# Input x loaded in column halves around the first weight slab, with matmuls of constants on TensorE until it is in

## The reference

```python
h = rmsnorm(x, norm_g) @ w_in            # x: 544 x 1024, w_in: 1024 x 3080
gb, gc, hv, q, k, v, fl = jnp.split(h, splits, axis=-1)
q = rmsnorm(q.reshape(bsz, t, N_HEADS_B, HEAD_DIM), q_g)
k = rmsnorm(k.reshape(bsz, t, N_HEADS_B, HEAD_DIM), k_g)
logf = jax.nn.log_sigmoid((fl + b_f).astype(jnp.float32))
# sample group: keys, values and log forgets of 16 pages per sequence come from paged pools
lf_all = jnp.concatenate([logf_pool[page_table].reshape(bsz, p_len, h), logf_new], axis=1)
c = jnp.cumsum(lf_all, axis=1)
```

## Time and profile before

| | |
|---|---|
| median of 3 runs | 1461.29 us (1457.95 to 1469.23) |
| span of the profiled execution | 1458.5 us |
| PE busy | 1395.5 us (96%) |
| DVE, ACT, POOL busy | 721.0, 488.2, 603.2 us |
| DMA | 191.60 MB, mean 131 GB/s |

### The profile page before, as it was taken

The page is one execution under the profiler, slowest core; times in us unless marked ns, Lnnn a source line. Parts: engine busy times, 40 slices in busy tenths (PEclk is TensorE's granted clock), DMA queues, the critical chain, the costliest instruction groups (busy, mean ns, idle before and its releaser), DMA issues.

```text
span 1458.5 us, 34454 instructions
## 1 busy us (share of the span) xinstructions
PE 1395.5 (96%) x13989; PEld 1303.2 (89%) x13989; DVE 721.0 (49%) x1258; ACT 488.2 (33%) x718; POOL 603.2 (41%) x337
## 2 busy tenths in 40 slices
PE   6998998988999999999999999998999999999998
PEld 5896767767899999999999998867999999999998
DVE  5646888873535444014443367667365430144411
ACT  4375333322233222312223352237433321222221
POOL 3322332322335554445543464432255554355431
PEclk9999999998999999999999999999999999999999
DMA  6417899978322322332312546642223223322122
GB/s 185 131 54 243 289 336 319 364 267 276 120 74 77 96 83 75 88 115 83 89 55 64 147 132 162 161 118 68 61 88 96 84 76 90 101 87 86 54 84 74
DMA packets 245642, 191.60 MB, mean 131 GB/s; under 512 B 11970, under 2 KB 204947, under 8 KB 245451
## 3 DMA queue, kind: packets, MB, share of 16 engines
q1 hardware_dynamic: 244273, 187.71, 42.0%
q0 software_dynamic: 656, 2.13, 0.5%
q10 hardware_dynamic: 605, 0.24, 0.1%
HBM read 173.03 MB, written 6.04 MB: 123 GB/s over the span
## 4 chain that ended last, share of the span: by engine, by line
PE 73%; DVE 3%; ACT 1%; issue 1%; POOL 1%; DMA 0%; DVEq 0%; ACTq 0%; POOLq 0%
PE banks L1823 65%; PE banks L2265 2%; PE banks L2089 1%; PE banks L1840 1%; PE banks L2211 1%; PE banks L2028 1%; DVE k_grp L1317 0%; PE banks L1970 0%; PE banks L2268 0%; POOL sb L706 0%; DMA u_sh<-u 0%; POOL u_sh L790 0%; PE banks L2217 0%; PE banks L1857 0%; PE banks L2061 0%
## 5 line engine op out<-in xcount | busy, mean ns | idle before, releaser
L685 POOL TENSOR_TENSOR w_l<-w_raw,w_h 128x1024 fp32r<-128x1024 f32 (+2 forms) x195 | 439.5, 2255 | 400.7 <-ACT w_h L835 380.7
L1823 PE MATMUL banks<-xa_h,w_h 128*128 128x272 f32 x1856 | 388.1, 290 | 4.1 <-DVE tmp L1650 3.3
L1823 PE MATMUL banks<-xa_h,w_l 128*128 128x272 f32 x1856 | 384.5, 289 | 0.0
L1823 PE MATMUL banks<-xa_l,w_h 128*128 128x272 f32 x1856 | 383.1, 288 | 0.0
L1823 PEld LDWEIGHTS banks<-xa_h,w_h 128*128 128x128 f32 x1856 | 293.0, 189 | 6.4 <-issue 5.0
L1823 PEld LDWEIGHTS banks<-xa_l,w_h 128*128 128x128 f32 x1856 | 292.3, 189 | 0.0
L1823 PEld LDWEIGHTS banks<-xa_h,w_l 128*128 128x128 f32 x1856 | 290.3, 189 | 0.0
L835 ACT ACTIVATE w_h<-w_raw 128x1024 fp32r<-128x1024 f32 (+2 forms) x193 | 185.2, 961 | 199.5 <-PE banks L1823 199.4
L1823 PE MATMUL banks<-h_h,w_h 128*128 128x272 f32 x928 | 193.5, 290 | 0.3 <-DVE x L1589 0.3
L1823 PE MATMUL banks<-h_h,w_l 128*128 128x272 f32 x928 | 192.8, 289 | 0.0
L1823 PE MATMUL banks<-h_l,w_h 128*128 128x272 f32 x928 | 192.2, 289 | 0.0
(11 more groups left out here) (301 smaller groups left out, 1667.9 us busy)
## 6 DMA issues: line engine op xcount, KB each, us to landing
w_raw<-in_w_up SPq DMA_DIRECT2D x88, 512.0 KB, 3.7
k_grp<-in_cache_k SPq DMA_DIRECT2D x128, 256.0 KB, 4.5
v_pg<-in_cache_v SPq DMA_DIRECT2D x120, 256.0 KB, 4.8
w_raw<-in_w_in SPq DMA_DIRECT2D x24, 512.0 KB, 6.4
w_raw<-in_w_down SPq DMA_DIRECT2D x32, 384.0 KB, 3.3
w_raw<-in_w_pw SPq DMA_DIRECT2D x24, 512.0 KB, 4.1
w_raw<-in_w_down SPq DMA_DIRECT2D x32, 320.0 KB, 3.2
w_raw<-in_w_out SPq DMA_DIRECT2D x8, 512.0 KB, 6.2
```

The lines of the kernel that those rows point to most:

```text
L685: g.tensor_tensor(w_l[:, slot, 0:n], w_raw[:, slot, 0:n], w_h[:, slot, 0:n].bitcast(F32), ALU.subtract).then_inc(s_lo, 1)
L1823: ins = mm(out[:, half, 0:HT], w, v[:, half * HT:(half + 1) * HT], start=first and t == 0 and n == 0, stop=last and t == phase.tiles - 1 a ...
```

## The change

x comes in two halves of its columns (chunks 0 to 3 and chunks 4 to 7), with the load of slab 0's weights between them; `pgix` and `a_row` are issued behind slab 1's weights. PE multiplies ones by ones into an idle part of bank 1: 9 matmuls once the ones are written, 4 behind the gain, 6 between the halves of x. Chunks 0 to 3 are turned when the first half is there, 4 and 5 ahead of slab 0, and 6 and 7 inside slab 0 ahead of its chunks 3 and 4. The first three slabs write three different pairs of banks, and the sums and the turned log forgets go to banks 6 and 7 (`sides`). POOL makes the low parts of slabs 0 to 2 and two of the eight squares (chunks 0 and 2); the sum over the channels moves from slab 1's chunk 4 to slab 2's chunk 1, the turning of `lf_pg` and `later_sums` from behind slab 1 to behind slab 2.

```diff
+SQUARED = (1, 3, 4, 5, 6, 7)
+AWAKE = (9, 4, 6)
...
-        x_turned = [banks[:, n:n + 2, :].rearrange("p k c -> p (k c)")[:, 0:T] for n in (0, 4, 2, 6)]
+        x_turned = [banks[:, n:n + 2, :].rearrange("p k c -> p (k c)")[:, 0:T] for n in (0, 4, 2, 6, 0, 2, 6, 0)]
+        sides = banks[:, 6:8, :]
+        idle_bank = banks[:, 1, 256:256 + P]
+        qkv_out = lambda n: (pair[1], pair[0], psum_s)[n] if n < 3 else pair[n % 2]
...
+            def x_half(half):
+
+                at = slice(half * D // 2, (half + 1) * D // 2)
+                for k in range(4):
+                    sp.dma_start(x_rows[:, k, at], a["x_prompt"][0, k * P:(k + 1) * P, at]).then_inc(s_xld[half], 16)
+                sp.dma_start(x_rows[0:TS, 4, at], a["x_sample"].rearrange("b t d -> (b t) d")[:, at]).then_inc(s_xld[half], 16)
+
+            x_half(0)
...
             for j in range(4):
                 load(ph["qkv"], 0, j, cols(w_in, 1536 + j * P))
+                if j == 0:
+                    x_half(1)
+                if j == 1:
+                    sp.dma_start(pgix[:, :], a["page_table"].rearrange("b (p a) -> (b p) a", a=1)).then_inc(s_ix, 16)
+                    sp.dma_start(a_row[:, :], a["state_conv_a"][0].rearrange("b t d -> (b t) d")).then_inc(s_st, 16)
             sp.dma_start(page_row[:, :], a["page_table"].rearrange("(a b) p -> a (b p)", a=1)).then_inc(s_pg, 16)
-            sp.dma_start(pgix[:, :], a["page_table"].rearrange("b (p a) -> (b p) a", a=1)).then_inc(s_ix, 16)
-            sp.dma_start(a_row[:, :], a["state_conv_a"][0].rearrange("b t d -> (b t) d")).then_inc(s_st, 16)
...
+            split_low(0, 0, DC)
+            split_low(0, 1, DC)
             pool.wait_ge(s_ix, 16)
             g.indirect_dma_start(out=lf_pg[:, :], out_offset=None,
                                  in_=a["cache_logf"][0].rearrange("n k h -> n (k h)"),
                                  in_offset=bass.IndirectOffsetOnAxis(ap=pgix[:, 0:1], axis=0)).then_inc(s_lf, 16)
-
...
-            pool.wait_ge(s_xlo, DC)
-            for slot in range(1, 3):
-                split_low(0, slot, DC)
+            for b in range(2):
+                pool.wait_ge(s_xlo, 2 * b + 1)
+                g.tensor_tensor(tmp[:, b, :], x[:, 2 * b, :], x[:, 2 * b, :], ALU.mult).then_inc(s_sqe, 1)
+            split_low(0, 2, DC)
...
             for m in range(DC):
                 act.wait_ge(s_tp, m + 1)
                 if m % 2:
-                    A(x[:, m, :], x_turned[m % 4], ACT.Copy).then_inc(s_xnew, 1)
-                A(xa_h[:, m, :], x_turned[m % 4], ACT.Copy, scale=par("mix0", m)).then_inc(s_xhi, 1)
-                if m == 1:
-                    split_high(0, 0, DC)
+                    A(x[:, m, :], x_turned[m], ACT.Copy).then_inc(s_xnew, 1)
+                A(xa_h[:, m, :], x_turned[m], ACT.Copy, scale=par("mix0", m)).then_inc(s_xhi, 1)
+                if m in (0, 3):
+                    split_high(0, m // 3, DC)
             act.wait_ge(s_xnew, DC)
-            for m in range(DC):
-                if m in (0, 3):
-                    split_high(0, 1 + m // 3, DC)
-                if m >= 2:
-                    act.wait_ge(s_ss, m)
-                A(sq[:, m % 2, :], x[:, m, :], ACT.Square).then_inc(s_sq, 1)
+            for n, m in enumerate(SQUARED):
+                if n == 1:
+                    split_high(0, 2, DC)
+                if n >= 2:
+                    act.wait_ge(s_ss, n + 2)
+                A(sq[:, n % 2, :], x[:, m, :], ACT.Square).then_inc(s_sq, 3 if n == len(SQUARED) - 1 else 1)
...
             for m in range(DC):
                 dve.wait_ge(s_xhi, m + 1)
                 if m % 2 == 0:
-                    V.tensor_copy(x[:, m, :], x_turned[m % 4]).then_inc(s_xnew, 1)
-                V.scalar_tensor_tensor(xa_l[:, m, :], x_turned[m % 4], par("mix0", m), xa_h[:, m, :].bitcast(F32),
+                    V.tensor_copy(x[:, m, :], x_turned[m]).then_inc(s_xnew, 1)
+                V.scalar_tensor_tensor(xa_l[:, m, :], x_turned[m], par("mix0", m), xa_h[:, m, :].bitcast(F32),
                                        ALU.mult, ALU.subtract).then_inc(s_xlo, 1)
-                if m == 3:
-                    dve.wait_ge(s_hi, 1)
-                    V.tensor_tensor(w_l[:, 0, :], w_raw[:, 0, :], w_h[:, 0, :].bitcast(F32), ALU.subtract).then_inc(s_lo, 1)
...
+            dve.wait_ge(s_sqe, 2)
+            V.tensor_tensor(ssum[:, :], tmp[:, 0, :], tmp[:, 1, :], ALU.add).then_inc(s_ss, 3)
+            def params_kept():
...
+            for n in range(len(SQUARED)):
+                if n == 4:
+                    params_kept()
+                dve.wait_ge(s_sq, n + 1)
+                dve.wait_ge(s_ss, n + 3)
+                V.tensor_tensor(ssum[:, :], ssum[:, :], sq[:, n % 2, :], ALU.add).then_inc(s_ss, 1)
+            inv_rms(0, 0, sides)
...
             for n in range(12):
-                scaled(qkv[:, n, :], n, n % 2)
-                if n == 1:
+                dve.wait_ge(s_slab, n + 1)
+                V.tensor_tensor(halves(qkv[:, n, :]), qkv_out(n)[:, :, 0:HT], halves(r_all[:, :]), ALU.mult).then_inc(s_free, 1)
+                if n == 2:
                     later_sums()
-                if n == 2:
                     selectors()
...
-                        before = order[order.index(phase) - 1]
-                        pe.wait_ge(s_xnew if before.residual else s_free, before.group1 - 1 + q)
+                if phase is order[0]:
+                    if g == 0:
+                        pe.wait_ge(s_xlo, 2)
+                        pe.wait_ge(s_xhi, 2)
+                    elif g >= 3:
+                        pe.wait_ge(s_free, {3: 1, 4: 2}.get(g, g - 1))
...
+            def kept_awake(n):
+
+                for _ in range(n):
+                    mm(idle_bank, ones[:, :], ones[:, :], start=True, stop=True)
+
+            def chunk_turned(m):
+
+                free = {4: 1, 5: 3, 6: 4, 7: 5}.get(m)
+                if free:
+                    pe.wait_ge(s_xlo, free)
+                    pe.wait_ge(s_xhi, free)
+                for t in range(4):
+                    tr(x_turned[m][:, t * P:(t + 1) * P], x_rows[:, t, m * P:(m + 1) * P], ident[:, :])
+                tr(x_turned[m][:, TP:T], x_rows[0:TS, 4, m * P:(m + 1) * P], ident[0:TS, 0:TS]).then_inc(s_tp, 1)
+
+            pe.wait_ge(s_cst, 2)
+            kept_awake(AWAKE[0])
             pe.wait_ge(s_cst, 15)
             pe.wait_ge(s_gin, 16)
             tr(bank[0][:, 0:DC], p_rows[0:DC, 0, :], ident[0:DC, 0:DC]).then_inc(s_gn, 1)
-            pe.wait_ge(s_xld, 16 * 5)
-            for m in range(DC):
+            kept_awake(AWAKE[1])
+            pe.wait_ge(s_xld[0], 16 * 5)
+            for m in range(4):
                 if m == 3:
                     pe.wait_ge(s_gnd, 1)
-                if m >= 4:
-                    pe.wait_ge(s_xlo, m - 3)
-                    pe.wait_ge(s_xhi, m - 3)
-                for t in range(4):
-                    tr(x_turned[m % 4][:, t * P:(t + 1) * P], x_rows[:, t, m * P:(m + 1) * P], ident[:, :])
-                tr(x_turned[m % 4][:, TP:T], x_rows[0:TS, 4, m * P:(m + 1) * P], ident[0:TS, 0:TS]).then_inc(s_tp, 1)
-
-            pe.wait_ge(s_xlo, 5)
+                chunk_turned(m)
+            pe.wait_ge(s_xlo, 1)
+            pe.wait_ge(s_xhi, 1)
+            kept_awake(AWAKE[2])
+            pe.wait_ge(s_xld[1], 16 * 5)
+            for m in range(4, 6):
+                chunk_turned(m)
...
+            def first_chunks(k):
+
+                if k in (3, 4):
+                    chunk_turned(k + 3)
+                pe.wait_ge(s_xlo, k + 1)
...
             def first_sums(k):
 
-                if k == 4:
+                if k == 1:
                     pe.wait_ge(s_ss, 9)
-                    sum_channels()
+                    pe.wait_ge(s_miscd, 2)
+                    sum_channels(sides)
...
             for n in range(12):
-                slab(p, n // 4, n % 4, xa, (lambda k: pe.wait_ge(s_xlo, k + 1)) if n == 0 else first_sums if n == 1 else None)
+                slab(p, n // 4, n % 4, xa, first_chunks if n == 0 else first_sums if n == 2 else None)
                 if n == 0:
                     params_turned()
-                if n == 1:
+                if n == 2:
```

More of the change, by code:

```diff
@@ L313, in build @@
         s_free = sem("free")
-        s_prm, s_xld, s_st, s_fw, s_ix, s_lf = (sem(n) for n in (
-            "params_in", "x_in", "state_in", "fw_in", "index_in", "logf_in"))
+        s_prm, s_st, s_fw, s_ix, s_lf = (sem(n) for n in (
+            "params_in", "state_in", "fw_in", "index_in", "logf_in"))
+        s_xld = [sem(f"x_in{half}") for half in range(2)]
+        s_sqe = sem("early_squares")
         s_cst = sem("constants")
@@ L418, in _ @@
         def _(sp):
-            for k in range(4):
-                sp.dma_start(x_rows[:, k, :], a["x_prompt"][0, k * P:(k + 1) * P, :]).then_inc(s_xld, 16)
-            sp.dma_start(x_rows[0:TS, 4, :], a["x_sample"].rearrange("b t d -> (b t) d")).then_inc(s_xld, 16)
```

(36 more changed lines are left out.)

33 lines of the change are left out of this document (14 added, 19 removed).

## The result

The changed kernel takes 1477.19 us (median of 15 runs, 1464.94 to 1481.71) against 1461.18 for the kernel before on the same chip (15 runs, 1452.65 to 1469.76): ratio 1.0099, 95% interval 1.0074 to 1.0124. The forecast was 1460.5, range 1451 to 1467: the time lies 10 us above its upper end.

A forecast was written before the change was run, and what follows sets the result against it. PE alone was taken to bound 56 to 120 us, the DMA stream 120 to 340. Terms -1.5 + 1.8 = +0.3 us gave 1458.8 against the span of 1458.5, stated as a median of 1460.5, range 1451 to 1467.

The forecast's parts named there:

- one event: Start of line 1924, at 52.40 us before; its shift was to price the whole change, forecast 50.9.
- an unforeseen shift in the DMA-bound stage: From 120 us on: the only thing said able to move the time over one per cent (14.6 us); 0.03 each side.
- Part 1: Loading x in halves: first half lands at 6.5 us instead of 9.4, bounds 6.0 and 9.4.
- Part 2: First slab: at full clock a chunk turns in 0.64 us and slab 0 ends at 21.1 us against 27.2.
- rival 2: Start of kernel: clock low when x comes, slab 0 ends at 26.2, 4.5 us slower, about 1465; chance 0.12.
- Part 3: Sums over the channels: PE starts them at 29.9 us against 33.45, 3.6 won; bounds 28 and 31.5.
- Part 4: Behind the sums to line 1924: page sums held by POOL's splits leave 1.5 us won; low clock costs 1.8.
- The sum of the four parts: Whole kernel: -1.5 us at line 1924 plus 1.8 for the low clock, +0.3 us; between -2.5 and +3.
- Rival 1: Page sums ahead of line 1924 run free of POOL's splits: line 8.1 us earlier, about 1452; chance 0.10.

The follow-up runs named there:

- the 44 products: Changed kernel plus 44 tiny unread products (176 PE instructions) inside PE's wait at line 1974: 1461.17 us, ratio 0.9995.

## Why the prediction was wrong

**The step that failed** is the first: "So whatever moves the first 56 us moves the rest by the same amount; the change is priced by one event". From 56 to 120 us that held to 0.1 us. Behind 120 us it did not, and the chance of 0.03 for "an unforeseen shift in the DMA-bound stage" was all that stood for it. It came from reading the attention as bound by its stream of keys and weights (0.92 of the DMAs). But PE is busy for 197.0 of the same 220 us, in bursts, and what stopped it in a burst lengthened the stage: 8.8 us of waits, and 7.2 us more stage than in the first profile of before, 11.8 more than in its second.

**The quantity that was not counted.** The prediction asks of the 19 products of constants only what they do to the clock. They are 76 PE instructions, with two more waits of the change 78, which move every later one in its block. By the sum of what the blocks lack, the kernel before stood at the best place there is, 0.2 us of it against 23.6 at the worst of the 256 shifts (23.4 at the one that was run); a shift could only lose. Moved back to a whole block, the changed kernel measures 1461.17 against 1460.87, and the forecast for it was 1460.5.

**Part 1** (x): landed at 7.74 (7.2 to 8.1 over the ten profiles where nothing else held PE), forecast 6.5 with bounds 6.0 and 9.4. **Part 2**: in this profile the clock stood at its upper level (2.4 GHz) when x came, so rival 2 fell here; in 2 of 11 profiles with the constants its low clock did come. Slab 0 ended at 23.1, 2.0 later than forecast: 1.2 from x; a turned chunk took 0.76 us and not 0.64, and PE waited twice for DVE's `xa_l` (1.1 and 0.5 us), of which the forecast had only a part. **Part 3**: the sums at 30.83, forecast 29.9 with bounds 28 and 31.5. **Part 4** held line by line: a wait of 0.73 for POOL ahead of slab 3 (forecast 0.8), additions behind five splits, line 1974 at 51.90 after 6.8 us of idling (50.9 and 6.6), and 0.57 granted behind it. Line 1974 is 0.50 us earlier than line 1924 was and the end of "qkv" 1.25 later: the low clock cost 1.75 (forecast 1.8). Over the seven profiles in which PE idles there the cost goes from 1.6 to 2.9 us, past the forecast's bound of 2, and the end of "qkv" of one and the same program moves by 1.3 us (118.8 to 120.1 for before, 120.0 to 121.2 for the changed kernel), so part of the agreement to a tenth is luck. The sum of the four parts came out at +1.25 for +0.3.

**Rival 1** (additions that run free) was the right counterpart. Its 8.1 us are what reading PSUM brought (8.6), and the rule of the Trainium skill ("SBUF — State Buffer", "Who interferes with whom") is borne out: one SBUF input, no contention, 0.30 us each beside a running split.

**The median.** The forecast set a span against times. In every run that lists both, the time is 1.7 to 1.9 us above the span, so the span of 1458.5 stands for about 1460.2, and the median of 1460.5 was not 2 us off it. 16 us measured, 17.0 between the two profiles. The blocks are 16.0 of the medians (undone by the 44 products) but 12.5 of the spans. The Conformer's 7.5 us stand in that profile, but that they belong to the change is not shown; the profiled execution of before won the tie that its repetition lost. One profile of each kernel would have laid half of the loss on the change. The 1.5 us of the second feed-forward part, with a dip of the clock at 1083 us, were not followed; they stand again in the changed kernel's second profile and in the three with the 44 products at line 1974, and in no other.

## What to carry to other kernels

Before adding or removing PE instructions ahead of a stage with bursts of short matmuls, count them: number all of PE's records in the trace, its sequencer's too, cut them into blocks of 256 at the marks where waits on issue turn up, and see which blocks would last less than 5 us. If a change that should be neutral costs a per cent far behind itself, and PE shows waits on "issue", pad the stream to a whole block before judging it. Chained additions with one operand in PSUM do not queue behind POOL's splits. Take a second profile before explaining a loss in a stage that the edit does not touch.

## What the hardware showed that I had not expected

- A short block of 256 PE instructions makes PE wait for the next. Of the 13 blocks in the attention that lasted less than 3 us, 12 had a wait behind them, 0.5 to 3.3 us, 2.1 in the middle; of 35 with 3 to 4.1 us, 21 (up to 3.0); of 146 with 4.1 to 5.5 us, 37 (up to 1.6); of 487 longer ones none over 0.15 us. The Trainium skill, "Runtime: NRT & Kernel Launch", section "Instruction fetch mechanics", tells of blocks of this size and calls the cost of crossing one "mostly hidden". The trace agrees on the size; on the cost it does not, where the block is a burst: 8 to 15 us in a stage of 266 to 277.
- At the shared port the one that starts first need not win: DVE's shift began 0.45 us ahead of the tap weights in both outcomes, and in one it was held for 7.58 us, over three instructions of POOL. The Trainium skill ("SBUF — State Buffer", "Who interferes with whom") says that issue order decides who blocks, and, of DVE's two-port modes, that whoever issues first has the pair for its whole instruction; by the records' start times, the row does not bear that out. What was issued first within them, the trace does not show.
- Two executions of one program can part for good at such a meeting, though the starts of both instructions, counted from the first `ua`, differ by no more than 0.03 us over all 15 profiles: 4 us of the Conformer in the kernel before.
- The MATMULs of constants ahead of the first transposes had the clock at 2.4 GHz for them in 9 of 11 profiles. In the other 2 the transposes ran at 1.2 GHz and slab 0 started 3 to 4 us later, though each has the same instructions up to there as a kernel of the 9.
